# RWKV scan in a two-layer hybrid decoder: VectorE takes up the previous chunk's state ahead of the first two steps of the transposed inverse

## What is computed

```
def step(S, inp):
    r_t, w_t, k_t, v_t, kk_t, b_t = inp
    sa = jnp.einsum('bhij,bhj->bhi', S, kk_t)
    S = S * w_t[:, :, None, :] - sa[..., None] * b_t[:, :, None, :] + v_t[..., None] * k_t[:, :, None, :]
    y = jnp.einsum('bhij,bhj->bhi', S, r_t)
    return S, y
```

## Time and profile before

| | before |
|---|---|
| median of 3 runs | 3873.41 us (3871.0 to 3877.73) |
| the profiled execution | 3878.44 us |
| its span in the trace | 3876.7 us |
| granted TensorE clock, mean over the span | 0.964 of full speed |
| first layer's scan | about 643 to 905 us |
| second layer's scan | about 2573 to 2838 us |

### The profile page before, as it was taken

The page is one execution under the profiler, slowest core; times in us unless marked ns, Lnnn a source line. Parts: engine busy times, 40 slices in busy tenths (PEclk is TensorE's granted clock), DMA queues, the critical chain, the costliest instruction groups (busy, mean ns, idle before and its releaser), DMA issues.

```text
span 3876.7 us, 68856 instructions
## 1 busy us (share of the span) xinstructions
PE 3607.6 (93%) x29056; PEld 2793.4 (72%) x29056; DVE 2040.2 (53%) x4091; ACT 914.9 (24%) x1775; POOL 563.4 (15%) x443
## 2 busy tenths in 40 slices
PE   7998987999979999999899998879999899999996
PEld 5565566997658888888655555669965688888885
DVE  2499655776153243434536986477751633434345
ACT  2336464332020000000124464633321100000000
POOL 0131100000022222222101311000000212222220
PEclk9999997999989999999999999979999899999997
DMA  3110100001111111112210100100011111111121
GB/s 121 32 37 28 55 20 7 4 4 62 45 61 44 44 44 44 44 44 88 73 57 27 41 28 28 29 15 4 4 73 38 66 44 44 40 37 44 44 88 55
DMA packets 44297, 165.26 MB, mean 43 GB/s; under 512 B 5552, under 2 KB 5584, under 8 KB 43632
## 3 DMA queue, kind: packets, MB, share of 16 engines
q1 hardware_dynamic: 28672, 102.82, 8.0%
q0 software_dynamic: 15344, 58.27, 4.1%
HBM read 134.50 MB, written 23.49 MB: 41 GB/s over the span
## 4 chain that ended last, share of the span: by engine, by line
PE 70%; DVE 9%; ACT 2%; issue 2%; POOL 0%; DVEq 0%; ACTq 0%; POOLq 0%
PE ps L749 40%; PE ps L775 11%; PE ps L688 6%; PE ps L656 6%; DVE arena L1478 1%; DVE arena L1374 1%; PE ps L946 1%; PE ps L934 1%; DVE arena L1381 1%; PE ps L959 1%; PE ps L666 1%; PE ps L700 1%; DVE arena L1570 1%; DVE arena L1568 0%; DVE arena L1845 0%
## 5 line engine op out<-in xcount | busy, mean ns | idle before, releaser
L749 PE MATMUL ps<-arena 128*128 128x261 f32 x4096 | 924.5, 383 | 2.9 <-POOL arena L574 2.9
L749 PEld LDWEIGHTS ps<-arena 128*128 128x128 f32 x4096 | 775.2, 189 | 131.8 <-issue 3.8
L688 PE MATMUL ps<-arena,ring 128*128 128x348 f32 x2304 | 699.0, 462 | 31.3 <-ACT arena L1124 17.6
L749 PE MATMUL ps<-arena,ring 128*128 128x261 f32 x3072 | 711.5, 387 | 16.9 <-DVE arena L1845 16.5
L749 PEld LDWEIGHTS ps<-arena,ring 128*128 128x128 f32 x3072 | 588.0, 192 | 120.2 <-issue 14.5
L688 PEld LDWEIGHTS ps<-arena,ring 128*128 128x128 f32 x2304 | 436.9, 192 | 294.4 <-issue 48.9
L775 PE MATMUL ps<-arena 64*64 64x64 f32 (+1 forms) x13600 | 476.9, 225 | 48.9 <-DVE arena L1570 23.6
L775 PEld LDWEIGHTS ps<-arena 64*64 64x64 f32 x13600 | 452.7, 136 | 69.0 <-DVE arena L1570 27.9
L1334 ACT ACTIVATE aux<-ps 128x522 f32<-128x522 f32 x64 | 38.9, 607 | 1527.8 <-PE ps L749 1527.8
L1420 DVE TENSOR_TENSOR arena<-aux,ps 128x522 f32<-128x522 f32 x160 | 111.8, 699 | 425.0 <-PE ps L749 424.5
L574 POOL TENSOR_TENSOR arena<-ring 128x512 f32<-128x512 f32 x128 | 173.6, 1356 | 1098.6 <-DMA ring<-units 1093.2
(11 more groups left out here) (223 smaller groups left out, 3435.7 us busy)
## 6 DMA issues: line engine op xcount, KB each, us to landing
ring<-units SPq DMA_DIRECT2D x192, 512.0 KB, 3.7
h_scratch<-arena POOLq DMA_DIRECT2D x24, 522.0 KB, 3.2
arena<-h_scratch POOLq DMA_DIRECT2D x24, 522.0 KB, 8.0
arena<-h_in POOLq DMA_DIRECT2D x16, 522.0 KB, 10.0
out<-arena POOLq DMA_DIRECT2D x8, 522.0 KB, 3.1
arena<-att_scratch POOLq DMA_DIRECT2D x2, 2080.0 KB, 9.1
att_scratch<-arena POOLq DMA_DIRECT2D x16, 256.0 KB, 3.0
aux<-rope POOLq DMA_DIRECT2D x2, 1044.0 KB, 12.1
```

Of the source, the lines that this page charges most:

```text
L688: ins = mm(ps[:, b + s, 0:SW], ring[:, r * D + k * P:r * D + (k + 1) * P], tile(U0, k)[:, slice_(s)], start=(k == 0), stop=(k == KT - 1))
L749: ins = mm(acc_at(n)[:, s], lhs[:, k * P:(k + 1) * P], rhs(k)[:, s * HALF:(s + 1) * HALF], start=(k == 0), stop=(k == KT // 2 - 1))
```

## The change

The two calls of `new_state` in `dve_chunk` are moved from behind the loop that makes MT at level 0 to ahead of it. Everything else stays, and so do all waits and signals.

```
                     dve.wait_ge(S["dve_done"], m_done)
                     v.tensor_tensor(m, m, over2(ident2), ALU.add).then_inc(S["m_ready"], 1)
+                if not first:
+                    new_state(w, 1 - odd, 0)
+                    new_state(w, 1 - odd, 1)
                 for half in range(2):

                     mt = half2("mt", half)
...
                         dve.wait_ge(S["u_mm"], w.next("u_mm"))
                     do(v.tensor_tensor(mt, half2("abt", half), over2(const("inv0t")), ALU.mult))
                     v.tensor_tensor(mt, mt, over2(ident2), ALU.add).then_inc(S["mt_ready"], 1)
-                if not first:
-                    new_state(w, 1 - odd, 0)
-                    new_state(w, 1 - odd, 1)
                 for n in range(1, LEVELS):
```

## The result

| | before | after |
|---|---|---|
| median of the runs compared | 3877.73 us (7 runs, 3870.96 to 3878.73) | 3886.98 us (7 runs, 3880.48 to 3889.19) |
| the profiled execution | 3878.44 us | 3886.98 us |
| its span | 3876.7 us | 3885.2 us |

The ratio is 1.0032, with a 95% interval of 1.0022 to 1.0042: the change makes the kernel slower by 0.32%, some 12 us (0.0032 x 3877.7). The forecast was 3891.6 us and 18.2 us slower. Sign and mechanism were right, the size was too large by a half.

A forecast was written before the change was run, and what follows sets the result against it. TensorE was taken as the bound. A slip of 0.57 us a chunk over 32 chunks gave 18.2 us, put on a median of 3873.4: 3891.6 us, range 3883 to 3898.

The forecast's parts named there:

- Step 1: On VectorE at a chunk boundary, the new state's halves start 1.41 and 2.64 us behind ScalarE's copy of u.
- Step 2: On VectorE, the second half of the state ends at 756.46, so the state is ready 0.42 us earlier.
- Step 3: MT on VectorE starts 0.42 us behind the last L1570, so TensorE resumes 0.32 us late in each chunk.
- Step 4: In VectorE's next work, L1622 follows L1605 by 0.42 us, updates 0.20 apart; the second M is 0.57 late.
- no slack stands behind the second M: TensorE's level 2 product already waits for the second M, so the 0.57 us slip goes whole into the chunk.
- the full slip: The whole lateness at the second M: 0.57 us a chunk, bounds 0.41 to 0.69, 13 to 22 us; chance 76%.
- the faster one: Rival: TensorE's matmuls are released by the state alone, 0.42 us earlier a chunk, 13.4 us less, 3860; chance 4%.
- TensorE's waits still name L1570: Sign of being wrong: in the profile after, TensorE was expected to wait for L1598 instead, about 1.05 us a chunk.
- chunks under 15.9: Sign of being wrong: scan chunks under 15.9 us apart, meaning slack at the second M; 16.2 was expected.
- The absorbed backlog: Rival: VectorE's lateness is absorbed, only TensorE's late start counts, 0.32 us a chunk, 10.2 us, 3883.7; chance 8%.
- The rival of instructions a full duration apart: VectorE instructions each stand their own duration apart; second M 0.67 us late, 21.4 us, 3894.8; chance 4%.
- The granted clock: Rival: TensorE's longer idle time in the scan makes its clock fall to half, past 3898 us; chance 3%.

The follow-up runs named there:

- e1: Kernel before with VectorE order state half 0, MT half 0, state half 1, MT half 1; ratio 0.9983, 3869.25 us beside 3875.73.
- e5: Kernel after's VectorE order, with TensorE rearranged to sum both new-state halves early and the rest of y last; ratio 0.9980, 3867.69 us beside 3875.62.
- e6: Kernel before's VectorE order, with TensorE rearranged to sum both new-state halves early and the rest of y last; ratio 0.9998, chunk 15.65 us.
- e3: Kernel before plus one unused 128 x 128 VectorE instruction behind the state, in front of L1605; chunk 15.65 to 15.68 us against 15.65.
- e4: Kernel after plus one unused VectorE instruction behind MT, in front of L1605; chunk 16.18 and 16.25 us by turns against 15.97 and 16.05.
- e7: Like e5 on TensorE; VectorE's eight state and MT instructions paired so none waits for the one right ahead; ratio 0.9946, 3854.16 us beside 3875.62.
- e2_around: Kernel before with VectorE order state half 0, both MT halves, state half 1; one run, 3867.9 us, chunk 15.70 us against 15.65.
- e8: Kernel before's TensorE order; VectorE weaves both MT halves with the state's first half, ahead of its second; ratio 0.9963, 3863.34 us.

## Why the prediction was right, and where it was off

Step 1 held to 0.01 us in its first half (1.41). The second start was forecast at 2.64 and came at 2.57 in one chunk and 2.64 in the next, by turns; that alternation is the whole difference between chunks of 15.97 and 16.05. Why it alternates was not tried. Step 2 held: the state is ready 0.41 to 0.48 earlier. The heart of the forecast, MT queued behind VectorE's wait for the second state, is what e1, e5 and e6 show: fill the hole or take the wait away, and the early state is a gain.

Step 3 was too dear by 0.10. I took 0.42 from the last L1570 to MT, and it is 0.32 (756.89 to 757.21), even a little below the lower bound of 0.33. I had reasoned that a change of counter costs 0.09; at this place it cost nothing.

Step 4 holds the largest error of reading. I took 0.42 from L1605 to L1622 as VectorE's own spacing. It was TensorE's pace: before the change VectorE was waiting a little for the products there. Its own spacing is 0.33, as after (758.28 to 758.61) and as e3 shows in the old order. That is another 0.09 too much. The 0.20 between updates was right (four starts from 758.61 take 0.20 to 0.21 each), and so was the claim that no slack stands behind the second M: e4's pad goes through in full. This term had no lower bound, and so 0.375 us a chunk lies below the 0.41 that I gave as the least of the full slip (12.0 us where I had 13). The forecast had VectorE's backlog add 0.25 to TensorE's late start (0.57 to 0.32); it adds 0.06 (0.33 to 0.27 in the chunk shown). Most of the loss is the late start, and the backlog comes last by little.

The sum again with the measured terms: 0.57 - 0.10 - 0.09 - 0.035 (half of the 0.07) = 0.345 us a chunk, beside 0.32 and 0.40 measured in mid-scan, 0.375 over the whole scan. Times 32, the forecast terms gave 18.2 us; the measured ones give 11.0, and the scan shows 12.0. That the time itself, 3886.98 us, came within 5 us of the forecast is in part luck: the forecast stood on a median before of 3873.4 from three executions, and the seven compared with gave 3877.7.

TensorE resumes 0.15 behind the end of MT's half 0, not 0.05 as it did behind the state (757.54 + 0.29 = 757.83, then 757.98). I had forecast 0.05. It did no harm, since VectorE sets the second M either way.

Of the rivals, the faster one (TensorE released by the state alone) fell: the state is earlier by what was worked out, and TensorE waits for MT. One of my signs of being wrong was that TensorE's waits still name L1570; the weight loads' row does, but by the times above it names an instruction that had ended 0.77 us before. The other, chunks under 15.9, did not come. The absorbed backlog could not be told from the forecast by the total (10.2 us, where 12.0 were measured); it fell with e4. The rival of instructions a full duration apart fell with the four updates, and again in e7: the starts are 0.20 to 0.21 apart, but for 0.27 between the two sums of the state, for which no run shows the reason. I had read only half of "VectorE: DVE Perf Modes" in the Trainium skill, section "The DRAIN you can't avoid": the same section says that an instruction which is not held starts earlier. The trace fits that half (what holds an instruction was not tried here): an instruction that does not wait for the one before starts 0.07 to 0.09 us before that one has ended. What this case does not bear out is that a semaphore between costs nothing: a wait for the one before costs 0.11 more (0.32 in place of 0.21). The granted clock stayed at 1.00 in the stretch with the longer idle time.

## What to carry to other kernels

To move work ahead on an engine that runs in order, ask first whether its input is there. Here the first half of the state was and the second was not, and everything behind the wait paid. Work that is ready belongs in front of a wait, cut finely enough to fill the hole and no more; and between instructions that need each other, put others that don't.

When you take a spacing from a trace as an engine's own, check that it wasn't waiting: two starts 0.42 apart, with a duration of 0.42, looked like one behind the other and were another engine's pace.

## What the runs showed of the hardware that was not expected

The time outside the scan differs between single executions by several us, though no kernel here changes the work there, and TensorE's granted clock goes with it. The 20 executions of the kernel before that stand beside e5 to e8 range from 3867.18 us, at a mean clock of 0.969, to 3878.57, at 0.965. The stretch from 600 to 660 us, ahead of and into the first chunks, in the kernel before and in e2_around:

```profile
600.00:660.00 60.00, 45.02 (x506) 31.79 (x508) 39.33 (x75) 22.19 (x33) 1.27 (x2) 0.66 0.03 10
```

```profile
600.00:660.00 60.00, 43.74 (x662) 33.07 (x660) 44.25 (x93) 24.25 (x40) 0.56 (x1) 0.77 0.04 10
```

The granted clock is 0.66 in one and 0.77 in the other (its levels are 1.2 and 2.4 GHz, that is 0.5 and 1), and the first copy of u comes at 659.3 in the one and at 653.0 in the other. That 6.3 us is half of what the change costs. It is also half of why e2's single total is below the kernel before although its chunks are longer: between the two scans e2 gains another 5.3 us, which was not taken apart. So a small change is better read from its own stage than from one total. Why the clock stays low for longer in some executions was not tried.

The 0.15 us with which TensorE resumes behind MT, beside 0.05 behind the state, stays open too: MT is what it loads as weights, and that load may be what adds the tenth, but no run took it apart.
